# PEER rows gathered per head and rank: 104 tokens with the token on the partition, first 20 row products on GpSimd

## The reference, cut to what matters

```python
q = jnp.matmul(xt, wq).reshape(t, 8, 2, 128)
scores = jnp.einsum('thcd,hcnd->thcn', q, sub_keys)
sv, si = lax.top_k(scores, 16)
cand_s = (sv[:, :, 0, :, None] + sv[:, :, 1, None, :]).reshape(t, 8, 256)
cand_i = (si[:, :, 0, :, None] * 128 + si[:, :, 1, None, :]).reshape(t, 8, 256)
best_s, best_p = lax.top_k(cand_s, 16)
idx = jnp.take_along_axis(cand_i, best_p, axis=-1)
gate = jax.nn.softmax(best_s, axis=-1)
act = jnp.einsum('td,thkd->thk', xb, u_tab[ib])       # dot with the chosen u rows
wgt = jax.nn.gelu(act) * gb
y = jnp.einsum('thk,thkd->td', wgt, v_tab[ib])        # weighted sum of the chosen v rows
```

## Time and profile before

| | |
|---|---|
| median of 3 runs | 2349.61 us (2344.91 to 2351.23) |
| profiled execution, its own time | 2351.88 us |
| its span in the trace | 2349.9 us |
| TensorE matmul busy | 2199.5 us (94%) |
| VectorE busy | 1209.5 us (51%) |
| ScalarE busy | 429.9 us (18%) |
| GpSimd busy | 470.2 us (20%) |
| moved by DMA | 616.38 MB, mean 262 GB/s |

### The profile page before, as it was taken

How to read it: one execution, slowest core, us unless ns; L and a number is a source line. 1 busy time by engine, 2 the same in 40 slices (tenths; PEclk the granted TensorE clock), 3 DMA queues, 4 the chain that set the end, 5 groups by cost and what they waited for, 6 DMA issues and landing times. The chain is left out here.

```text
span 2349.9 us, 32587 instructions
## 1 busy us (share of the span) xinstructions
PE 2199.5 (94%) x13344; PEld 1962.8 (84%) x13344; DVE 1209.5 (51%) x2470; ACT 429.9 (18%) x1034; POOL 470.2 (20%) x410
## 2 busy tenths in 40 slices
PE   4999779998998999999999998998999999999998
PEld 2466468887667899999999998667899999999998
DVE  2045521112532597887744443542597787844443
ACT  2113320000232112442200000232112443200000
POOL 0000000000000012554433331000012444533331
PEclk7999989999987999999999999997999999999999
DMA  8216213343331378999999995431378999999996
GB/s 334 74 71 249 108 54 142 136 153 135 143 135 54 144 268 338 384 384 392 410 409 409 395 406 222 181 144 54 120 257 338 382 392 386 407 409 409 407 406 252
DMA packets 113525, 616.38 MB, mean 262 GB/s; under 512 B 10201, under 2 KB 10585, under 8 KB 95322
## 3 DMA queue, kind: packets, MB, share of 16 engines
q1 hardware_dynamic: 55578, 403.31, 43.8%
q0 software_dynamic: 57504, 208.82, 23.2%
q10 hardware_dynamic: 288, 2.10, 0.3%
HBM read 612.16 MB, written 2.03 MB: 261 GB/s over the span
## 5 line engine op out<-in xcount | busy, mean ns | idle before, releaser
L390 PE MATMUL psum<-HT,arena 128*128 128x160 f32 (+1 forms) x5984 | 994.3, 327 | 15.5 <-DVE HT L1632 7.1
L390 PEld LDWEIGHTS psum<-HT,arena 128*128 128x128 f32 x5984 | 925.5, 192 | 68.7 <-issue 18.1
L390 PE MATMUL psum<-arena 128*128 128x160 f32 (+6 forms) x5850 | 882.2, 313 | 36.4 <-DMA arena<-in_peer_v 14.4
L390 PEld LDWEIGHTS psum<-arena 128*128 128x128 f32 (+2 forms) x5850 | 817.1, 193 | 85.9 <-issue 32.3
L1950 DVE SCALAR_TENSOR_TENSOR arena<-arena,small 128x1024 f32<-128x1024 f32 x180 | 231.2, 1285 | 293.2 <-DMA arena<-in_peer_v,small 285.9
L2050 POOL DMA_INDIRECT arena<-in_peer_u,small x192 | 245.7, 1279 | 317.7 <-DVE small L1901 280.9
L2050 POOL DMA_INDIRECT arena<-in_peer_v,small x192 | 210.6, 1097 | 357.9 <-PE psum L390 209.3
L1901 DVE CUSTOM_DVE_ANT_0 arena<-arena 128x1024 f32<-128x1024 f32 x192 | 228.1, 1221 | 51.6 <-DMA arena<-in_peer_u,small 45.8
L2056 POOL DMA_DIRECT2D row_tokens<-arena x2 | 1.2, 624 | 1118.9 <-ACT arena L957 1118.9
L390 PE MATMUL psum<-arena,HT 128*128 128x384 f32 (+3 forms) x544 | 202.8, 533 | 17.6 <-ACT HT L1009 10.7
L390 PEld LDWEIGHTS psum<-arena,HT 128*128 128x128 f32 x544 | 108.1, 201 | 105.4 <-issue 48.5
(11 more groups left out here) (226 smaller groups left out, 1003.7 us busy)
## 6 DMA issues: line engine op xcount, KB each, us to landing
arena<-in_peer_ut SPq DMA_DIRECT2D x64, 2048.0 KB
arena<-in_peer_v SPq DMA_DIRECT2D x64, 2048.0 KB
arena<-in_w_mod SPq DMA_DIRECT2D x12, 2048.0 KB
arena<-in_w_in SPq DMA_DIRECT2D x16, 1536.0 KB
arena<-in_w_up SPq DMA_DIRECT2D x11, 2048.0 KB
arena<-in_peer_wq SPq DMA_DIRECT2D x8, 2048.0 KB
arena<-in_w_out SPq DMA_DIRECT2D x6, 2048.0 KB
arena<-in_w_down SPq DMA_DIRECT2D x11, 1024.0 KB
```

The lines of the kernel that those rows point to most:

```text
L390: return pe.matmul(o, a, b, start=start, stop=stop, skip_group_check=True)
```

## The change

- `ROW_TOKENS` goes from 96 to 104, so `TD` goes from 160 to 152, and the gathered tokens are now the first ones of block 0 instead of the last ones of block 1. `choose` runs block 0 first.
- A buffer holds one head and one rank of all 104 tokens, with the token on the partition: 128 gathers of 104 rows per table and layer. The ring has 10 buffers. The expert numbers are written where they are used (`EG`), the gates are copied on chip (`GG`), and the DRAM round trips and `spread_rows` go. The gathers start after the first `choose` (its `idx_ready`).
- The dots of the first 20 buffers are a product on GpSimd (`row_product`), in place in the buffer, and a sum on ScalarE (`row_sum`), one after the activation of each pair from the second on. GpSimd issues a further gather after each product from the third on. VectorE starts at buffer 20.
- The v gathers follow TensorE with four per tile used. There is one `row_values`, after all v tiles, with the identity in place of the selection matrix.
- The gated part starts at pair 23 with 38 groups (before: 22 and 40), the selections follow pair 20 (before: 19). The `xn` transposes move between the query jobs, the sub-scores of block 0 go first.

```diff
-ROW_TOKENS = 96
+ROW_TOKENS = 104
 TD = T - ROW_TOKENS
-GTOK = P // PH
-RGROUPS = ROW_TOKENS // GTOK
-ROWS = RGROUPS * TOPK
-RING = 8
+ROWS = NSEL
+RING = 10
...
-FIRST_GATED = 22
-DOTS_BEFORE, DOTS_NUM = 9, 4
-EXP_AFTER, SELECT_AFTER = 16, 19
+FIRST_GATED = 23
+POOL_ROWS, SUM_LAG = 20, 1
+DOTS_BEFORE, DOTS_NUM = 29, 4
+EXP_AFTER, SELECT_AFTER = 16, 20
...
-                def row_values(g):
-
-                    pe.wait_ge(s("yp_ready"), g + 1)
+                def row_values():
+
+                    pe.wait_ge(s("yp_ready"), 1)
                     for m in range(KC):
-                        c = (m % 2) * T + TD + g * GTOK
-                        last = mm(psum[4 + m // 2][:, c:c + GTOK], YP[g % 4][:, m * P:(m + 1) * P], SELG,
-                                  False, g == RGROUPS - 1)
-                        if g == RGROUPS - 1 and m % 2 == 1:
+                        c = (m % 2) * T
+                        last = mm(psum[4 + m // 2][:, c:c + ROW_TOKENS], YP[0:ROW_TOKENS, m * P:(m + 1) * P],
+                                  IDENT[0:ROW_TOKENS, 0:ROW_TOKENS], False, True)
+                        if m % 2 == 1:
                             end(last, f"y{m // 2}")
...
-                due = [(g + 1) * XQ // RGROUPS + 2 for g in range(RGROUPS - 1)]
                 for q in range(XQ):
                     expert_values(q)
-                    if q in due:
-                        row_values(due.index(q))
-                row_values(RGROUPS - 1)
+                row_values()
...
+                def row_sum(n):
+
+                    rows = GR[n % RING][0:ROW_TOKENS, :]
+                    act.wait_ge(s("row_product"), n + 1)
+                    act.activation(rows, rows, ACT.Copy, accum_out=ACTV[0:ROW_TOKENS, n:n + 1]
+                                   ).then_inc(s("row_summed"), 1)
+
                 for m in range(PAIRS_U):
                     expert_activations(m)
+                    if 0 <= m - SUM_LAG < POOL_ROWS:
+                        row_sum(m - SUM_LAG)
...
-                    if b == 1:
+                    if b == 0:
...
+                        dve.tensor_copy(EG[:, own].bitcast(U32), BA[:, own]).then_inc(s("idx_ready"), 1)
...
-                for t in range(4):
-                    choose(1, t)
-                for t in range(4):
-                    choose(0, t)
+                            dve.scalar_tensor_tensor(y, rows, w, y, ALU.mult, ALU.add).then_inc(rows_used, 1)
+                        dve.wait_ge(rows_used, m + 1 - POOL_ROWS)
+
+                for b in range(TB):
+                    for t in range(4):
+                        choose(b, t)
...
-                row_dots(0, 2)
...
-                row_dots(2, DOTS_BEFORE - 2)
+                dve.wait_ge(s("gate_ready"), 1)
+                dve.tensor_copy(GG, GATE[:, 0:NSEL]).then_inc(s("gate_kept"), 1)
+                row_dots(POOL_ROWS + 2, DOTS_BEFORE - POOL_ROWS - 2)
...
-                dve.wait_ge(s("gate_moved"), layer * 32 + 32)
-                for g in range(RGROUPS):
-                    own = slice(g * TOPK, (g + 1) * TOPK)
-                    dve.wait_ge(s("row_acts"), g + 1)
-                    steps(dve.tensor_tensor(ACTV[:, own], ACTV[:, own], GG[:, own], ALU.mult))
-                    row_sums(g * TOPK, TOPK)
+                dve.wait_ge(s("gate_kept"), 1)
+                jobs.wait_full(dve, f"g{GBATCHES - 1}")
+                for h in range(PH):
+                    own = ACTV[0:ROW_TOKENS, h * TOPK:(h + 1) * TOPK]
+                    dve.wait_ge(s("row_acts"), h + 1)
+                    steps(dve.tensor_tensor(own, own, GG[0:ROW_TOKENS, h * TOPK:(h + 1) * TOPK], ALU.mult))
+                    row_sums(h * TOPK, TOPK)
+                dve.sem_inc(s("yp_ready"), 1)
...
                         j = m % RING
-                        if m >= RING:
-                            pool.wait_ge(rows_used, m - RING + 1)
+                        if RING <= m < RING + POOL_ROWS:
+                            pool.wait_ge(s("row_summed"), m - RING + 1)
+                        elif m >= RING:
+                            pool.wait_ge(rows_used, m - RING - POOL_ROWS + 1)
+                        if m < ROWS and m % (2 * TOPK) == 0:
+                            pool.wait_ge(s("idx_ready"), m // (2 * TOPK) + 1)
                         if m >= ROWS + VALUE_LEAD:
                             pool.wait_ge(s("v_used"), (m - ROWS - VALUE_LEAD) // (ROWS // XQ) + 1)
-                        if m < ROWS and m % TOPK == RING - 1 and TOPK < m < (RGROUPS - 1) * TOPK:
-                            spread_rows(m // TOPK + 1)
                         pool.indirect_dma_start(
-                            out=GR[j], out_offset=None, in_=rows, in_offset=bass.IndirectOffsetOnAxis(
-                                ap=EG[:, n:n + 1].bitcast(U32), axis=0)).then_inc(gathered[j], 16)
-
+                            out=GR[j][0:ROW_TOKENS, :], out_offset=None, in_=rows,
+                            in_offset=bass.IndirectOffsetOnAxis(
+                                ap=EG[0:ROW_TOKENS, n:n + 1].bitcast(U32), axis=0)).then_inc(gathered[j], 16)
...
+                def row_product(n):
+
+                    j = n % RING
+                    rows = GR[j][0:ROW_TOKENS, :]
+                    pool.wait_ge(gathered[j], layer * slot_uses(j) + (n // RING + 1) * 16)
+                    pool.sem_inc(tick, 1)
+                    pool.tensor_tensor(rows, rows, XNS[0:ROW_TOKENS, :], ALU.mult).then_inc(s("row_product"), 1)
+
+                gathers("peer_u_2", 0, RING)
                 for half in range(2):
...
+                for n in range(POOL_ROWS):
+                    row_product(n)
+                    if n >= 2:
+                        gathers("peer_u_2", RING + n - 2, 1)
+                gathers("peer_u_2", RING + POOL_ROWS - 2, ROWS - RING - POOL_ROWS + 2)
                 gathers("peer_v_2", ROWS, ROWS)
```

More of the change, by code:

```diff
@@ L282, in build @@
         PROD = take(4, 256)
-        BA, BB, BP, BV, BI, BJ, GATE, EIDX = (take(TB * NSEL) for _ in range(8))
-        XNS = take(D)
+        BA, BB, BP, BV, BI, BJ, GATE = (take(TB * NSEL) for _ in range(7))
         assert a_at[0] <= wa_at + XTILES * TD
@@ L287, in build @@
         GR = [SQF[:, n * D:(n + 1) * D] for n in range(4)] + [take(D) for _ in range(RING - 4)]
-        XNG = take(2, D)
+        XNS = take(D)
         oh_at = a_at[0]
         OH = take(4, BATCH, P)
-        SELT = take(3, T)
-        YP = [view(oh_at, D), view(oh_at + D, D), XNG[:, 0, :], XNG[:, 1, :]]
-        EG, GG, ACTV = (small[:, n * ROWS:(n + 1) * ROWS] for n in range(3))
+        SELT = take(3, TD)
+        KEYS = view(oh_at, 16 * NK)
+        YP = view(oh_at, D)
+        EG, ACTV = (small[:, n * ROWS:(n + 1) * ROWS] for n in range(2))
+        GG = CP2[:, C2["vng"]:C2["vng"] + ROWS]
         steps_act, steps_dve = sem("steps_act"), sem("steps_dve")
@@ L855, in _ @@
                         if t:
-                            sub_scores(t - 1, 1 - j)
+                            sub_scores(t - 1, j)
+                    if t == 1:
+                        for half in range(2):
+                            transposes(f"xn{half}", [HT[:, 4 * half + j, 0:ROW_TOKENS] for j in range(4)],
+                                       rows=ROW_TOKENS)
+                sub_scores(3, 0)
                 sub_scores(3, 1)
-                sub_scores(3, 0)
                 def expert_scores(q):
@@ L1207, in _, with row_activations @@
                         if t:
-                            sub_scores(t - 1, 1 - j)
-                sub_scores(3, 1)
[L1210 to L1214, removed]
+                            sub_scores(t - 1, j)
+                    if t == 1:
+                        for half in range(2):
+                            copy_out(f"xn{half}", XNS[0:ROW_TOKENS, half * 512:(half + 1) * 512],
+                                     bank(f"xn{half}")[0:ROW_TOKENS, :])
+                sub_scores(3, 0)
+                sub_scores(3, 1)
+                def row_activations(h):
+                    act.wait_ge(s("row_summed"), min((h + 1) * TOPK, POOL_ROWS))
+                    if (h + 1) * TOPK > POOL_ROWS:
+                        act.wait_ge(rows_used, (h + 1) * TOPK - POOL_ROWS)
+                    own = ACTV[0:ROW_TOKENS, h * TOPK:(h + 1) * TOPK]
                     act.activation(own, own, ACT.Gelu_apprx_tanh).then_inc(s("row_acts"), 1)
@@ L1891, in choose @@
                         steps(dve.tensor_scalar(BA[:, own], BA[:, own], base[:, 0:1], None, ALU.add))
-                        dve.tensor_copy(EIDX[:, own].bitcast(U32), BA[:, own]).then_inc(s("idx_ready"), 1)
+                        dve.tensor_copy(EG[:, own].bitcast(U32), BA[:, own]).then_inc(s("idx_ready"), 1)
                 def row_dots(first, count):
                     for n in range(first, first + count):
-                        g, j = n // TOPK, n % RING
-                        if n % TOPK == 0:
```

(14 more changed lines are left out.)

86 lines of the change are left out of this document (23 added, 63 removed).

## The result

The changed kernel takes 2904.55 us (median of 4 runs, 2885.62 to 2912.24), the kernel before 2350.42 (4 runs): ratio 1.233, 95% interval 1.229 to 1.238. The prediction was 2325 us, faster. The profiled execution took 2885.62 us, its span is 2883.8.

What follows compares the result with a forecast made beforehand. TensorE (94% busy) was taken as the bound, with DMA's limit near 405 GB/s lying on it. u 20.3 and 22.9 us less, v 6.9 and 11.3 more: -25.0 us, so 2325 us; range 2300 to 2370.

Steps and rivals of the forecast that it cites:

- 121.5 MB, at 405 GB/s 300.0 us: v stage: DMA carries this load at the assumed ceiling and becomes the bound, where it was 284 us.
- its 2 to 17: End of v stage: tail in us after DMA ends, put at 8, between 2 and 17.
- 378 GB/s, under 405: Gated pairs in u: 1.90 MB in 5.03 us stays under DMA's ceiling, so stalls mostly go.
- Rival 1: Gathers: 104 rows cost DMA as much as 128, the fullest path setting the pace; 2403 us, chance 0.20.
- rival 3: u stage: GpSimd's product is slow, 6.5 us, costing 53 us more a layer; 2431 us, chance 0.04.
- Tables and gathers take equal engine time a byte: v stage DMA, evidence against gathers costing by fullest path: 63.66 MB at 56.7%, 51.11 at 45.1%.
- Rival 2: Gathers: 104 rows divide unevenly over 16 engines and count as 112; 2347 us, no change, chance 0.13.
- (a): TensorE in u and v: 152 columns for 160, 6.7 ns less an instruction, 13.7 us less in each stage.
- (b): TensorE in u: two gate groups fewer, 2 x 0.89 = 1.8 us less.
- (c): TensorE in v: six row_values of 1.70 us become one of 1.8 us, 8.4 us less.
- 2.3 taken: GpSimd in u: assumed product time in us, giving a 4.2 us step hidden behind pairs of 4.14.
- VectorE may be 9 us later: Gates in u: ready at 911.8 us, while TensorE reaches the new selections at 920.8, leaving this slack.

Runs made afterwards that it cites:

- e8: Changed kernel with all gathers of 128 rows and no products on GpSimd or row sums on ScalarE, VectorE doing all 128 dots: 2457.98 us.
- e7: Kernel before with its v table tiles loaded into 104 of 128 partitions, gathers unchanged at 128 rows: 2618.77 us.
- e1: Changed kernel with every row gather made of 128 rows instead of 104: 2458.18 us, 1.048 times the kernel before.
- e3: Changed kernel with the v gathers alone cut to 64 rows, written to partitions 0 to 63: 2709.68 us.
- e10b: Changed kernel with the v gathers alone cut to 64 rows, written to partitions 32 to 95: 2516.59 us.
- e11: Kernel before with its v table tiles loaded into partitions 0 to 63 only, gathers of 128 rows unchanged: 2361.69 us.
- e12: Kernel before with its v table tiles loaded into partitions 32 to 95 only, gathers of 128 rows unchanged: 2323.57 us.
- e2: Changed kernel with every row gather made of 112 rows instead of 104: 2813.21 us, 1.198 times the kernel before.

## Why the prediction was wrong

**The failed step** is the price of a gather in the v stage: "121.5 MB, at 405 GB/s 300.0 us". The 405 GB/s had been read from transfers over 128 partitions, and it holds for those. The DMA view of the changed kernel's v stage, 1213.5 to 1731.4 us:

```profile
DMA packets 37815, 128.64 MB, mean 248 GB/s; under 512 B 6472, under 2 KB 6472, under 8 KB 37791
```

128.64 MB at 248 GB/s are the 518 us; at 409 GB/s they would be 315. The bytes were 7 MB over the forecast, mostly since late gathers left some 21 of u for v where it counted 10 (the gathers' queue moved 63.58 MB, 149 gathers). The tail after the last transfer was some 13 us, inside its 2 to 17. But the gathers that trail the last tile were not four: 26 were issued after 1660 us, and the last tile ended at 1663.6. The same step fails in u, where 1.90 MB in 5.03 us were to need "378 GB/s, under 405"; at 264 GB/s a pair needs 7.2 us, and u was 385.5 us for 299.7, with 15 to 25 us of it from the late gates (e8).

**What stands in its place**: a transfer into 104, 112, 96 or the lower 64 partitions keeps its engines busy (share 1.03, 0.92 in e7) and moves 201 GB/s (104 rows) or 252 (112) alone, 246 to 288 beside full ones, which it slows too. Each 4 KB then takes 0.32 us of an engine's time (104 rows), where full gathers take 0.17 (e1, 1480 to 1490 us), so the time is lost in the transfers and not between them. A transfer into 128 partitions, or into the 64 from 32 to 95, moves at 373 to 410. That is shown for gathers and for plain loads; e3 and e10b differ in the place alone, e11 and e12 also in which table rows they read. How it comes about is argued, with pages. The Trainium skill, DMA: Bandwidth & Descriptors, section Why a DMA increments its semaphore by 16 and not by 1, takes as the number of engines the largest up to 16 that divides the rows, so 13 for 104. The trace of e7 agrees for plain loads: by the starts and durations of its DMA packets exactly 13 are in flight in 34% of 1300 to 1500 us, in the kernel before (1180 to 1300 us) in under 2%. That an engine's rows follow one another, 8 each, is my assumption. The Trainium skill, SBUF — State Buffer, section Door 1: The DMA port swizzle, has a path for every 4 partitions, the same one again 32 further on, and other paths from partition 64 on. Taken together, the parts that start at 0 and 32, at 8 and 40, and so on begin on the same path, two engines to one, and half the lower paths rest; for 64 rows from 0 the engines meet in pairs too, and from 32 each has its own. No row shows an engine's path. The doubled price alone (2.12 us for 104/128 of 1.32) and e10b agree with it; the 252 GB/s of 112 rows only roughly. 104 rows from another start partition were not tried.

**Rival 1** named the right object and gave it 0.20, but its reason was how many rows the fullest path gets, which can't cost more than a full gather. Its sum, 2403 us, belongs to e1, which measured 2458: 128 rows in the same layout. No rival's price reaches the measured time (the highest is rival 3's 2431). What rival 1 misses, if the account above holds, is that engines can meet on a path at the same time. "Tables and gathers take equal engine time a byte" spoke against it; this was seen on transfers of 128 partitions only. **Rival 2**, 2347 us, fell with e2, where the rows divide evenly and the rate is 288.

**What held.** (a) and (b): pairs of 4.14 us (74.57 for 18) and 5.03, as computed; with full gathers and no products (e8) u was 299.1 us against 299.7 forecast, though with 37 dots left over instead of 17. (c): one row_values at the end, 1.93 us at a granted clock of 1.00 (e3), but 3.74 in the changed kernel, which had waited 64 us and had 0.50, the 1.2 GHz level; the 1.8 forecast left that wait out. GpSimd's product took 2384 ns against 2.3 taken, and its step hid behind the pairs, as said, so rival 3 is out.

**What failed besides.** "VectorE may be 9 us later" was true, but it was 18, and TensorE came to the selections at 915 us and not at 921: I had costed GpSimd's products by their own time and not by what they do to VectorE's. It is 15 us of waiting a layer (25 in u, by e8), and about nothing in sum, since with full gathers DMA sets when v ends. And 128 gathers a layer in v instead of 96 cost about what the bytes say: e1 moved 138.67 MB in v, the kernel before 115.87, which is 55.7 us at 409 GB/s, less some 6 for a shorter tail; v is 48.6 us longer. With that the 554 us are: 446 for the shape of the gathers (e1), about 97 for the larger number of full ones, the rest for u (late gates less TensorE's savings: 324.3 us for 320.0).

## To carry to other kernels

A DMA rate read from a profile belongs to the shape of the transfers that made it: before cutting a transfer to fewer partitions, or moving it to others, expect to lose rate for everything beside it, and look for the full share with fewer GB/s. Here it was far cheaper to move 24 useless rows than to leave them out; to save bytes, shorten rows and keep all 128 partitions (or 32 to 95). Where two engines do two-input work in SBUF at the same time, cost the slower one's effect on the faster.

## Not expected of the hardware

- Bytes left out made the time longer: 104 rows 2.12 us a gather, 128 rows 1.32, alone and with full queues.
- The same 64-row gather: 270 GB/s over partitions 0 to 63, 410 over 32 to 95.
- Each 104-row gather leaves 144 packets, as one of 128 rows does, 40 of them under 512 B instead of 16 (24185 small packets in all for 11897 in e1, over 512 gathers); 112 and 96 rows leave 16, and are slow too, so the small packets aren't the cause.
- VectorE's 512-column product beside GpSimd: up to 7.96 us for 0.69.
